# Where the last reciprocal roots of an RMSNorm are computed: on VectorE behind each tile, or on GpSimd between tiles

## The chip, the core and the metric

The kernel runs on one core of a Trainium2 chip (trn2). The metric is the time of one execution on the device, in microseconds. The core has five engines that run their own instruction streams and meet at semaphores: TensorE (PE, with its weight loads as PEld), VectorE (DVE), ScalarE (ACT), GpSimd (POOL) and SyncE (SP, which here only issues transfers). GpSimd issues transfers too.

## What is computed

One layer with a token-mixing half and an MLP half, 1024 tokens by 1024 channels, all in float32. The change touches only the last two lines, and of them only the end:

```python
def rmsnorm(x, g):
    y = x * lax.rsqrt(jnp.mean(x * x, axis=-1, keepdims=True) + EPS)
    return y * g

h = rmsnorm(x, g_mlp_pre)
f = jnp.square(jax.nn.relu(h @ w_up)) @ w_down
x = x + rmsnorm(f, g_mlp_post)
```

## The kernel before

Everything is written by hand: each engine's stream is a Python block, and each wait names a semaphore and a count. The tokens stand in eight tiles of 128 rows. The product with `w_down` is accumulated over the hidden channels in the on-chip tile `acc` (128 x 8 x 1024). The last slice of hidden channels is multiplied in at the very end, in 16 products of a tile `t` with a half of 512 output columns `s`, in the order of the list `LAST_DOWN`: (0,0), (1,0), (2,0), (0,1), (1,1), (2,1), and then (3,0), (3,1), (4,0) and so on to (7,1). This text calls them product 0 to product 15. Each is 12 matmuls on PE into one of eight banks.

For each product the other engines do the following.

- DVE adds the bank to `acc` (the **add**, line 2033), then writes `acc * 32 * gain` to a buffer of weighted values (the **mul**, line 2038). The buffer is `yx`, a view of `yst`, with room for two tiles.
- ACT squares the same half of `acc` and sums the squares of a row into a column of `sumsq` (line 1242). It is started by the add.
- When both halves of a tile are there, DVE computes the reciprocal root of the row's sum of squares: an integer seed and three Newton steps on columns of one or two numbers per partition (the **root**, lines 2010 to 2019). Each instruction waits for the one before it. Tiles 0 to 5 are done in pairs, tiles 6 and 7 singly; all of this is the function `finish`.
- DVE then writes `weighted * root + x1` into a third of `tok` (the **out**, line 2024). The residual `x1` of tile `t` has been brought there by a transfer that GpSimd issues (`x1_load`, line 767). There are three such places, so that the load for tile `t` waits until the output of tile `t - 3` has been sent (`out_sent`).
- SP sends the tile to the output (line 577). The last tile's out and its transfer are in two halves.

PE never waits for any of this in the last 16 products, since a bank is free again long before it comes round.

Of the kernel before, what the change touches and what calls it, by code (L numbers as in the profile page):

```python
# [17 lines left out]
D = 1024  # L18
L = 1024
KT = D // P  # L20
NT = L // P
# [8 lines left out]
EPS = 1e-6  # L30
# [26 lines left out]
RSQRT_SEED = float(0x5F3759DF)  # L57
# [63 lines left out]


LAST_DOWN = [(0, 0), (1, 0), (2, 0), (0, 1), (1, 1), (2, 1)] + [(t, s) for t in range(3, 8) for s in range(2)]


UP_PRODUCTS = [("uP1", 0, 0), ("uP2", 1, 1), ("uP6", 3, 2), ("uP5", 2, 3), ("uP7", 4, 0), ("uP3", 5, 1), ("uP4", 6, 2)]
# [33 lines left out]
def hybrid_layer(nc, a, out):  # L160
    f32, f32r, i32 = mybir.dt.float32, mybir.dt.float32r, mybir.dt.int32
    ALU, ACT, AX = mybir.AluOpType, mybir.ActivationFunctionType, mybir.AxisListType
    add, sub, mul = ALU.add, ALU.subtract, ALU.mult
    ctx = ExitStack()
    with ctx:
# [3 lines left out]
        def sem(name):  # L169
            return ctx.enter_context(nc.semaphore(name))  # L170
# [10 lines left out]
        stat = sb("stat", [P, 8])  # L181
        rs = sb("rs", [P, 10])
        sumsq = sb("sumsq", [P, 40])
        mx = sb("mx", [P, 64])
# [7 lines left out]
        raw = sb("raw", [P, 2, UNIT])  # L192
# [5 lines left out]
        tok = sb("tok", [P, 4096])  # L198
        yst = sb("yst", [P, 4, 512])
# [132 lines left out]
        sq_f = sem("sq_f")  # L332
# [8 lines left out]
        third_in = [sem(f"third_in{h}") for h in range(2)]  # L341
        turn_used = sem("turn_used")
        step_made, step_hi, step_lo, step_out = sem("step_made"), sem("step_hi"), sem("step_lo"), [sem(f"step_out{k}") for k in range(2)]
        x1_back = [sem(f"x1_back{s}") for s in range(3)]
        out_made, out_sent = sem("out_made"), [sem(f"out_sent{s}") for s in range(3)]
        chain = sem("chain")
# [127 lines left out]
        def loaded(slot, u, it):  # L474

            return w_loaded[slot], 16 * (2 * ((u - U_QX) // 2 + 1) + 2) + it * 64


        @block.sync
# [107 lines left out]
        def _(pool):  # L587

            g = nc.gpsimd
# [102 lines left out]
            yx = yst[:, :, :].rearrange("p (s a) c -> p s (a c)", s=2)  # L692
# [73 lines left out]
            def x1_load(t):  # L766
                g.dma_start(tok[:, (1 + t % 3) * D:(2 + t % 3) * D], x1_dram[tile_of(t) * P:(tile_of(t) + 1) * P, :]).then_inc(x1_back[t % 3], 16)
# [3 lines left out]
            x1_load(2)  # L771
            pool.wait_ge(f_lo, 8 + 42 + 4)
            x1_load(0)
            for t in range(3, NT):
                pool.wait_ge(out_sent[t % 3], 16 * (t // 3))
                x1_load(t)


        @block.scalar
# [467 lines left out]
        def _(dve):  # L1247
            V = nc.vector
            issued = [0]

            def mark(ins):

                issued[0] += 1
                ins.then_inc(chain, 1)

            def settle():

                dve.wait_ge(chain, issued[0])

            def do(ins):  # L1260
                mark(ins)
                settle()
# [71 lines left out]
            for e in range(2):  # L1334
                for idx in range(2):
                    n = norm_event(idx, e)
# [63 lines left out]
            for i, e in enumerate(X_ORDER):  # L1400
                n = FIRST["xsc"] + i
# [6 lines left out]
                                       in1=m2.unsqueeze(2).to_broadcast([P, 2, MEM]), op0=mul, op1=sub).then_inc(bank_free[n % 8], 1)  # L1408
# [34 lines left out]
            for i in range(2, 7):  # L1443
                rope(i)
                if i > 4:
                    n = FIRST["kv"] + i - 3
# [4 lines left out]
            for q in range(8):  # L1451
                for m in range(2):
                    n = FIRST["xpv"] + pv_event(q, m)
# [7 lines left out]
            for e in range(16):  # L1461
# [4 lines left out]
                n = score_event(e)  # L1466
                j = e % 2
# [5 lines left out]
                for lo, hi, nk in parts:  # L1473
# [4 lines left out]
                                          scalar=SS, in1=sk, op0=mul, op1=ALU.max))  # L1478
                for lo, hi, nk in parts:
                    ins = V.scalar_tensor_tensor(out=pe4[:, lo:hi, 0:nk], in0=ps[:, lo:hi, 0:nk], scalar=SS,  # L1480
                                                 in1=m4[:, lo:hi].unsqueeze(2).to_broadcast([P, hi - lo, nk]), op0=mul, op1=sub)
# [33 lines left out]
            for k in (1, 2, 4):  # L1515
                o = [pwF[:, ri, :, k + 1:2 * k + 1] for ri in range(2)]
                x = [pwF[:, ri, :, 1:k + 1] for ri in range(2)]
                y = [pwF[:, ri, :, k].unsqueeze(2).to_broadcast([P, NPAIR, k]) for ri in range(2)]
                t = [tt[:, 0:NPAIR * k].rearrange("p (a b) -> p a b", b=k) for tt in temps]
# [31 lines left out]
            for q in range(8):  # L1551
                n = FIRST["spv"] + spv_event(q, 2)
# [32 lines left out]
            for r in range(4):  # L1585
# [22 lines left out]
                for k in range(1, 7):  # L1608
                    w = 1 << k
# [5 lines left out]
                for e in range(2):  # L1615
                    n = FIRST[f"s5a{r}"] + 4 + e
                    wait_full(dve, n)
                    q = slice(2 * e, 2 * e + 2)
                    w = [banks[n % 8][:, :].rearrange("p (a ri c) -> p ri a c", a=2, ri=2)[:, ri] for ri in range(2)]
                    t = [tt[:, 256 * e:256 * e + 256].rearrange("p (a b) -> p a b", a=2) for tt in temps]  # L1620
# [19 lines left out]
                for e in range(2):  # L1640
                    n = FIRST[f"s5m{r}"] + e
                    dve.wait_ge(s5_even, 2 * r + e + 1)
                    for m in range(4):
# [3 lines left out]
                        ins = V.scalar_tensor_tensor(out=dst, in0=odd, scalar=parity[rows, 1:2], in1=dst, op0=mul, op1=add)  # L1647
# [6 lines left out]
                for e in range(2):  # L1654
                    n = FIRST[f"s5y{r}"] + e
# [19 lines left out]
            for e in range(8):  # L1675
                n = FIRST["yg"] + e
# [4 lines left out]
            for s in range(2):  # L1681
                prep_lo(dve, U_MERGE_A + s + 1)
                for j in range(8):
                    n, d, h = FIRST["mergeA"] + 8 * s + j, 4 * s + j // 2, slice((j % 2) * 512, (j % 2) * 512 + 512)
# [10 lines left out]
            for s in range(2):  # L1695
                prep_lo(dve, U_GLU + s + 1)
                for j in range(4):
                    n = FIRST["glu"] + 8 * s + 2 * j
                    h = slice((j % 2) * 512, (j % 2) * 512 + 512)
# [12 lines left out]
            for b, (stage, u) in enumerate((("mergeM", U_MERGE_M), ("mergeS", U_MERGE_S))):  # L1712
                dve.wait_ge(merged, 16 * (b + 1))
                for s in range(2):
                    prep_lo(dve, u + s + 1)
                    for j in range(8):
                        n, d, h = FIRST[stage] + 8 * s + j, 4 * s + j // 2, slice((j % 2) * 512, (j % 2) * 512 + 512)
# [63 lines left out]
            def step(i):  # L1781

                which, half = STEPS[i]
                b11, b12, b21, b22 = ([quarter(y, k, t, half) for y in (hThi, hTlo)] for k in range(2) for t in range(2))
                out, t2 = step_sum(i), tok_part[half]
                if which == S_T3:
                    do(V.tensor_tensor(out, b22[0], b12[0], sub))
                    do(V.tensor_tensor(out, out, b22[1], add))
                    V.tensor_tensor(out, out, b12[1], sub).then_inc(step_made, 1)
                elif which == S_T2:  # L1790
                    dve.wait_ge(step_lo, half + 1)
                    do(V.tensor_tensor(out, out, b11[0], add))
                    V.tensor_tensor(out, out, b11[1], add).then_inc(step_made, 1)
                else:
                    dve.wait_ge(step_lo, i)
                    first, then = (b22 if which == S_T1 else b21)
                    if i < 5:
                        dve.wait_ge(step_out[1], 32)
                    do(V.tensor_tensor(out, first, t2, sub))
                    V.tensor_tensor(out, out, then, add).then_inc(step_made, 1)  # L1800
# [200 lines left out]
                down_phase(m)  # L2001
            up_phase(6, True)

            def finish(tiles):

                c, n = slice(tiles[0], tiles[-1] + 1), len(tiles)
                v, nv, y, w = (stat[:, 2 * k:2 * k + n] for k in (0, 1, 2, 3)) if n == 1 else \
                    (stat[:, 0:2], stat[:, 2:4], rs[:, 0:2], stat[:, 4:6])
                dve.wait_ge(sq_f, LAST_DOWN.index((tiles[-1], 1)) + 1)
                do(V.scalar_tensor_tensor(out=v, in0=sumsq[:, 26:34][:, c], scalar=D * EPS, in1=sumsq[:, 10:18][:, c], op0=add, op1=add))  # L2010
                mark(V.tensor_scalar(nv, v, -0.5, None, mul))
                do(V.tensor_scalar(y.bitcast(i32), v.bitcast(i32), -0.5, RSQRT_SEED, mul, add))
                for _ in range(3):
                    if n == 1:
                        do(V.scalar_tensor_tensor(out=w, in0=y, scalar=nv, in1=y, op0=mul, op1=mul))
                    else:
                        do(V.tensor_tensor(w, y, y, mul))
                        do(V.tensor_tensor(w, w, nv, mul))
                    do(V.scalar_tensor_tensor(out=y, in0=w, scalar=1.5, in1=y, op0=add, op1=mul))
                for k, t in enumerate(tiles):  # L2020
                    xt = tok[:, (1 + t % 3) * D:(2 + t % 3) * D]
                    dve.wait_ge(x1_back[t % 3], 16 * (t // 3 + 1))
                    for h in ([slice(0, D)] if t < NT - 1 else [slice(0, 512), slice(512, D)]):
                        V.scalar_tensor_tensor(out=xt[:, h], in0=yx[:, t % 2, h], scalar=y[:, k:k + 1], in1=xt[:, h], op0=mul, op1=add)\  # L2024
                            .then_inc(out_made, 1)

            dve.wait_ge(last_gain, 16)
            n_last = F + 24
            for i, (t, s) in enumerate(LAST_DOWN):
                n, h = n_last + i, slice(s * 512, s * 512 + 512)  # L2030
                wait_full(dve, n)
                a = acc[:, tile_of(t), :]
                V.tensor_tensor(a[:, h], banks[n % 8][:, :], a[:, h], add).then_inc(bank_free[n % 8], 1)  # L2033
                wait_taken(dve, n)
                if (t, s) == (2, 0):
                    continue
                h = slice(0, D) if t == 2 else h
                mark(V.scalar_tensor_tensor(out=yx[:, t % 2, h], in0=a[:, h], scalar=float(D) ** 0.5, in1=tok[:, h],
                                            op0=mul, op1=mul))
                if s == 1 and t in (1, 3, 5):  # L2040
                    finish((t - 1, t))
                elif s == 1 and t > 5:
                    finish((t,))


        @block.tensor
# [491 lines left out]
```

## Time and profile before

| | |
|---|---|
| median of three runs | 1471.96 us (1471.65 to 1472.15) |
| span of the profiled execution, first to last instruction | 1470.3 us |
| its own time beside the span | not listed apart; the runs' median is 1.7 us above the span |
| granted TensorE clock over the span | 0.998 of full speed |
| first of the 16 last products begins, last one ends (PE) | 1416.50 us, 1460.28 us |
| last add begins on DVE | 1463.11 us |

All moments in this document are microseconds from the start of the span of the profiled execution. A row of the timeline gives the start, the duration, the engine and the line, what is written and what is read, and in brackets how long the engine had been idle and what ended that. "L2033" is line 2033 of the kernel before. An instruction that waits for nothing can start before the one ahead of it has wholly ended, so that the distance between starts is a little less than the duration.

### The profile page before, as it was taken

Reading aid. Unit: us, or ns where it says so; the run is one execution under the profiler, and the core shown is the slowest. Engines: PE = TensorE matmul, PEld = TensorE weight load, DVE = VectorE, ACT = ScalarE, POOL = GpSimd, SP = SyncE. Lnnn points to the kernel's source line nnn. Section 1 sums busy time; section 2 is a strip of 40 time slices with the busy share of each in tenths; the row PEclk is TensorE's granted clock in tenths of the full one; section 3 lists DMA queues with packets and bytes.
Section 4 is the critical chain, followed back from the end, with each engine's and each line's share of the span. In section 5 each row is a group of like instructions: output and inputs, shape, how many; then the busy total and the mean of one; then the engine's idle time right before and its main releaser. Section 6 shows DMA issues by size and latency. Waiting matters only on the chain.

```text
span 1470.3 us, 18474 instructions
## 1 busy us (share of the span) xinstructions
PE 1453.1 (99%) x7110; PEld 1210.6 (82%) x7110; DVE 1077.3 (73%) x1754; ACT 537.9 (37%) x697; POOL 198.8 (14%) x299
## 2 busy tenths in 40 slices
PE   8999999999999999999999999999999999999997
PEld 7888888888888888888898888888888888888885
DVE  6778668658757735446756869697969697978878
ACT  4445853323132253221234432333334343434332
POOL 0000010140211112101100212302020201011110
PEclk9999999999999999999999999999999999999999
DMA  8301120242213246424433436937372736464545
GB/s 329 73 29 58 58 87 29 100 130 95 73 64 107 65 135 206 146 68 133 172 102 113 129 115 207 308 114 229 98 242 88 228 115 208 134 180 145 168 165 186
DMA packets 113890, 199.65 MB, mean 136 GB/s; under 512 B 15224, under 2 KB 57248, under 8 KB 113824
## 3 DMA queue, kind: packets, MB, share of 16 engines
q0 software_dynamic: 46256, 118.53, 25.6%
q1 hardware_dynamic: 67552, 80.23, 16.5%
q8 instruction: 43, 0.70, 0.2%
q14 instruction: 23, 0.19, 0.0%
q10 hardware_dynamic: 16, 0.00, 0.0%
HBM read 163.08 MB, written 35.65 MB: 135 GB/s over the span
## 4 chain that ended last, share of the span: by engine, by line
PE 92%; DVE 5%; DMA 1%; issue 1%; ACT 1%; DVEq 0%; SPq 0%; ACTq 0%
PE bank L2056 53%; PE bank L2465 17%; PE bank L2485 14%; PE bank L2066 3%; PE bank L2096 1%; PE bank L2158 1%; DMA raw<-in_w_down_dram 1%; DVE tok L2024 1%; PE bank L2321 1%; PE bank L2306 1%; PE bank L2326 1%; PE bank L2291 1%; PE bank L2208 1%; PE bank L2263 1%; DVE acc L2033 1%
## 5 line engine op out<-in xcount | busy, mean ns | idle before, releaser
L2056 PE MATMUL bank<-hThi,whi 128*128 128x512 f32 x736 | 289.4, 393 | 0.1
L2056 PE MATMUL bank<-hThi,wlo 128*128 128x512 f32 x736 | 286.6, 389 | 0.0
L2056 PE MATMUL bank<-hTlo,whi 128*128 128x512 f32 x736 | 286.5, 389 | 0.0
L2056 PEld LDWEIGHTS bank<-hThi,whi 128*128 128x128 f32 x736 | 138.1, 188 | 30.1 <-issue 1.1
L1125 ACT ACTIVATE whi<-raw 128x1024 fp32r<-128x1024 f32 x91 | 95.3, 1055 | 183.4 <-DVE raw L1860 97.8
L2056 PEld LDWEIGHTS bank<-hThi,wlo 128*128 128x128 f32 x736 | 138.1, 188 | 29.2
L2056 PEld LDWEIGHTS bank<-hTlo,whi 128*128 128x128 f32 x736 | 138.2, 188 | 27.9
L1850 DVE TENSOR_TENSOR wlo<-raw,whi 128x1024 fp32r<-128x1024 f32 x91 | 111.0, 1220 | 33.6 <-ACT whi L1125 33.6
L2465 PE MATMUL bank<-hThi,whi 128*128 128x512 f32 x336 | 130.8, 389 | 0.5 <-DMA hTlo<-h_scratch 0.5
L2485 PE MATMUL bank<-whi,yhi 128*128 128x512 f32 x336 | 130.8, 389 | 0.4 <-DVE acc L1883 0.4
L2465 PE MATMUL bank<-hThi,wlo 128*128 128x512 f32 x336 | 130.7, 389 | 0.0
L2465 PE MATMUL bank<-hTlo,whi 128*128 128x512 f32 x336 | 130.7, 389 | 0.0
L2485 PE MATMUL bank<-whi,ylo 128*128 128x512 f32 x336 | 130.7, 389 | 0.0
L2485 PE MATMUL bank<-wlo,yhi 128*128 128x512 f32 x336 | 130.7, 389 | 0.0
L378 ACT ACTIVATE whi<-raw 128x2048 fp32r<-128x2048 f32 x32 | 61.2, 1916 | 102.8 <-PE bank L2056 70.3
L384 DVE TENSOR_TENSOR wlo<-raw,whi 128x2048 fp32r<-128x2048 f32 x33 | 75.5, 2290 | 18.1 <-ACT whi L378 17.4
L1883 DVE TENSOR_TENSOR acc<-bank,acc 128x1024 f32<-128x1024 f32 x72 | 86.1, 1218 | 1.0 <-PE bank L2485 1.0
L924 ACT ACTIVATE scr<-bank 128x512 f32<-128x512 f32 x48 | 28.5, 598 | 157.0 <-PE bank L2056 141.9
L2465 PEld LDWEIGHTS bank<-hThi,whi 128*128 128x128 f32 x336 | 63.1, 188 | 14.1 <-DMA hTlo<-h_scratch 0.9
L2485 PEld LDWEIGHTS bank<-whi,yhi 128*128 128x128 f32 x336 | 63.0, 188 | 13.8 <-DVE acc L1883 0.8
L2485 PEld LDWEIGHTS bank<-whi,ylo 128*128 128x128 f32 x336 | 63.1, 188 | 13.2
L2465 PEld LDWEIGHTS bank<-hThi,wlo 128*128 128x128 f32 x336 | 63.1, 188 | 13.1
(412 smaller groups left out, 2764.8 us busy)
## 6 DMA issues: line engine op xcount, KB each, us to landing
hThi<-h_scratch POOLq DMA_DIRECT2D x42, 512.0 KB, 5.3
hTlo<-h_scratch POOLq DMA_DIRECT2D x42, 512.0 KB, 6.5
raw<-in_w_in_dram SPq DMA_DIRECT2D x34, 512.0 KB, 4.7
raw<-in_w_up_dram SPq DMA_DIRECT2D x32, 512.0 KB, 4.2
raw<-in_w_down_dram SPq DMA_DIRECT2D x32, 512.0 KB, 4.5
gate_scratch<-scr POOLq DMA_DIRECT2D x48, 256.0 KB, 2.3
tok<-gate_scratch POOLq DMA_DIRECT2D x24, 512.0 KB, 3.6
yhi<-h_scratch POOLq DMA_DIRECT2D x14, 512.0 KB, 5.8
```

Source lines behind the costliest of these rows:

```text
L378: nc.scalar.activation(parts(u)[0], raw[:, u % 2, :], ACT.Copy).then_inc(w_hi, 1)
L384: nc.vector.tensor_tensor(lo, raw[:, u % 2, :], hi.bitcast(f32), sub).then_inc(w_lo, 1)
L924: A.activation(scr[:, gp % 2, :], banks[n % 8][:, :], ACT.Sigmoid).then_inc(bank_free[n % 8], 1)
L1125: A.activation(w_slot(whi, place), source, ACT.Copy).then_inc(w_hi, 1)
L1850: V.tensor_tensor(w_slot(wlo, place), source, w_slot(whi, place).bitcast(f32), sub).then_inc(w_lo, 1)
L1883: V.tensor_tensor(dst[:, 2 * h:2 * h + 2, :], pair_banks(k), dst[:, 2 * h:2 * h + 2, :], add).then_inc(pair_free[k], 1)
L2024: V.scalar_tensor_tensor(out=xt[:, h], in0=yx[:, t % 2, h], scalar=y[:, k:k + 1], in1=xt[:, h], op0=mul, op1=add)\
L2033: V.tensor_tensor(a[:, h], banks[n % 8][:, :], a[:, h], add).then_inc(bank_free[n % 8], 1)
L2056: ins = T.matmul(dst, lhs(k)[p], rhs(k)[q], start=start and k == 0 and i == 0, stop=stop and k == kt - 1 and i == 2)
L2066: ins = T.transpose(banks[n % 8][:, i * P:i * P + P] if dsts is None else dsts[i], src, by)
L2465: ins = T.matmul(banks[2 * k + c][:, :], w[:, kk, c * P:c * P + P], x[:, kk, :], start=opens and kk == 0 and i == 0, stop=kk == 3 and i == ...
L2485: ins = T.matmul(banks[2 * k + t % 2][:, :], x[:, kk, rows], w[:, kk, :], start=opens and kk == 0 and i == 0, stop=kk == 1 and i == 2, ski ...
```

## The change

There are three parts.

1. The roots of tiles 0 to 6 are computed by GpSimd (`make_root`), in groups of tiles (0, 1), (2, 3), (4, 5) and (6). Each is 15 instructions, and each of these waits on the semaphore `root_step` for the one before it. Their numbers stand in columns of `mx`. GpSimd's stream has one order: the first two groups, the loads of `x1` for tiles 3, 4 and 5, the third group, the load for tile 6, the fourth group, the load for tile 7. Tile 7's root stays on DVE.
2. Weighted values of tiles 2 to 5 go to the weight buffer `raw`, which is free by then; tiles 0, 1, 6 and 7 stay in `yst`. Tile 2 is multiplied in two halves rather than in one piece.
3. The outs are set between products by the table `OUT_AFTER`: tile 0 after product 6, tile 1 after 7, tile 2 after 9, tile 3 after 10, tile 4 after 12, tile 5 after 13, tile 6 after 14. Each waits for its `x1` and for `root_step` to reach 15, 30, 45 or 60.

```diff
+ROOTS = [(0, 1), (2, 3), (4, 5), (6,)]
+ROOT_STEPS = 15
+OUT_AFTER = {6: 0, 7: 1, 9: 2, 10: 3, 12: 4, 13: 5, 14: 6}
...
+        def last_rows(t):
+
+            return yst[:, 2 * (t % 2):2 * (t % 2) + 2, :].rearrange("p a c -> p (a c)") if t < 2 or t > 5 else \
+                raw[:, (t - 2) // 2, (t % 2) * D:(t % 2) * D + D]
...
-            for t in range(3, NT):
+            def step(ins):
+
+                roots[0] += 1
+                ins.then_inc(root_step, 1)
+                pool.wait_ge(root_step, roots[0])
+
+            def make_root(k):
+
+                tiles = ROOTS[k]
+                v, nv, y, w = root(k)
+                c = slice(tiles[0], tiles[-1] + 1)
+                pool.wait_ge(sq_f, LAST_DOWN.index((tiles[-1], 1)) + 1)
+                step(g.tensor_tensor(v, sumsq[:, 26:34][:, c], sumsq[:, 10:18][:, c], add))
+                step(g.tensor_scalar(v, v, D * EPS, None, add))
+                step(g.tensor_scalar(y.bitcast(i32), v.bitcast(i32), -0.5, RSQRT_SEED, mul, add))
+                for _ in range(3):
+                    step(g.tensor_tensor(w, y, y, mul))
+                    step(g.tensor_tensor(w, w, v, mul))
+                    step(g.tensor_scalar(w, w, -0.5, 1.5, mul, add))
+                    step(g.tensor_tensor(y, w, y, mul))
+
+            def x1_again(t):
+
                 pool.wait_ge(out_sent[t % 3], 16 * (t // 3))
                 x1_load(t)
+
+            make_root(0)
+            make_root(1)
+            x1_again(3)
+            x1_again(4)
+            x1_again(5)
+            make_root(2)
+            x1_again(6)
+            make_root(3)
+            x1_again(7)
...
-                if (t, s) == (2, 0):
-                    continue
-                h = slice(0, D) if t == 2 else h
-                mark(V.scalar_tensor_tensor(out=yx[:, t % 2, h], in0=a[:, h], scalar=float(D) ** 0.5, in1=tok[:, h],
-                                            op0=mul, op1=mul))
-                if s == 1 and t in (1, 3, 5):
-                    finish((t - 1, t))
-                elif s == 1 and t > 5:
-                    finish((t,))
+                mark(V.scalar_tensor_tensor(out=last_rows(t)[:, h], in0=a[:, h], scalar=float(D) ** 0.5, in1=tok[:, h], op0=mul, op1=mul))
+                if i in OUT_AFTER:
+                    done = OUT_AFTER[i]
+                    k = done // 2
+                    dve.wait_ge(root_step, ROOT_STEPS * (k + 1))
+                    settle()
+                    out_rows(done, root(k)[2][:, done % 2:done % 2 + 1])
+            y7 = last_root(NT - 1)
+            settle()
+            out_rows(NT - 1, y7)
```

How DVE's stream stands in the built programs, around the outs of tiles 4 and 5. Here L2024 is the out, L2033 the add, L2038 the mul, and L2017 to L2019 the end of a root. Before:

```order
L2017 TENSOR_TENSOR stat<-rs 128x2 [waits chain]
L2018 TENSOR_TENSOR stat<-stat 128x2 [waits chain]
L2019 SCALAR_TENSOR_TENSOR rs<-stat,rs 128x2 [waits chain]
L2024 SCALAR_TENSOR_TENSOR tok<-yst,rs,tok 128x1024 [waits x1_back1,chain]
L2024 SCALAR_TENSOR_TENSOR tok<-yst,rs,tok 128x1024 [waits x1_back2]
L2033 TENSOR_TENSOR acc<-bank,acc 128x512 [waits bank_full5]
L2038 SCALAR_TENSOR_TENSOR yst<-acc,tok 128x512 [waits bank_free5]
L2033 TENSOR_TENSOR acc<-bank,acc 128x512 [waits bank_full6]
L2038 SCALAR_TENSOR_TENSOR yst<-acc,tok 128x512 [waits bank_free6]
```

In the changed program the out is L2074, the add L2083 and the mul L2085; this is the stream from product 12 to product 14:

```order
L2083 TENSOR_TENSOR acc<-bank,acc 128x512 [waits bank_full5]
L2085 SCALAR_TENSOR_TENSOR yst<-acc,tok 128x512 [waits bank_free5]
L2074 SCALAR_TENSOR_TENSOR tok<-raw,mx,tok 128x1024 [waits x1_back1,chain,root_step]
L2083 TENSOR_TENSOR acc<-bank,acc 128x512 [waits bank_full6]
L2085 SCALAR_TENSOR_TENSOR yst<-acc,tok 128x512 [waits bank_free6]
L2074 SCALAR_TENSOR_TENSOR tok<-raw,mx,tok 128x1024 [waits x1_back2,chain,root_step]
L2083 TENSOR_TENSOR acc<-bank,acc 128x512 [waits bank_full7]
L2085 SCALAR_TENSOR_TENSOR yst<-acc,tok 128x512 [waits bank_free7]
L2074 SCALAR_TENSOR_TENSOR tok<-yst,mx,tok 128x1024 [waits x1_back0,chain,root_step]
```

The root's instructions have left DVE; each out now stands alone behind an add and a mul, and waits for `root_step`, which GpSimd counts up.

GpSimd's stream from the load of tile 0's `x1` on, before (L767 is `x1_load`):

```order
L767 DMA tok<-x_scratch 128x1024 [waits f_lo]
L767 DMA tok<-x_scratch 128x1024 [waits out_sent0]
L767 DMA tok<-x_scratch 128x1024 [waits out_sent1]
L767 DMA tok<-x_scratch 128x1024 [waits out_sent2]
L767 DMA tok<-x_scratch 128x1024 [waits out_sent0]
L767 DMA tok<-x_scratch 128x1024 [waits out_sent1]
```

And in the changed program, from the end of the second group of roots to the beginning of the third (L785 is `x1_load`, L807 to L814 a root):

```order
L813 TENSOR_SCALAR mx<-mx 128x2 [waits root_step]
L814 TENSOR_TENSOR mx<-mx 128x2 [waits root_step]
L785 DMA tok<-x_scratch 128x1024 [waits out_sent0,root_step]
L785 DMA tok<-x_scratch 128x1024 [waits out_sent1]
L785 DMA tok<-x_scratch 128x1024 [waits out_sent2]
L807 TENSOR_TENSOR mx<-sumsq 128x2 [waits sq_f]
L808 TENSOR_SCALAR mx<-mx 128x2 [waits root_step]
L809 TENSOR_SCALAR mx<-mx 128x2 [waits root_step]
L811 TENSOR_TENSOR mx<-mx 128x2 [waits root_step]
```

The loads of `x1` now stand behind roots in GpSimd's one stream, and the third root stands behind a load that waits for the output of tile 2.

## Rows read from the trace of the kernel before

**Rows 1.** Windows: busy time of each engine in stretches of the end.

```profile
core 0: us, PE busy (x) PEld busy (x) DVE busy (x) ACT busy (x) POOL busy (x), PEclk, DMA share, GB/s
1430.00:1440.00 10.00, 10.00 (x46) 8.29 (x45) 9.05 (x21) 2.17 (x6) 0.53 (x1) 1.00 0.29 111
1440.00:1450.00 10.00, 10.00 (x46) 8.29 (x45) 9.41 (x23) 2.90 (x8) 1.59 (x3) 1.00 0.65 231
1450.00:1460.00 10.00, 10.00 (x46) 8.18 (x44) 9.21 (x27) 2.17 (x6) 0.53 (x1) 1.00 0.60 209
```

**Rows 2.** Timeline of PE: the first and the last matmuls of the 192.

```profile
1416.50 0.47 PE L2056 MATMUL bank<-whi,yhi 128*128 128x512 f32 x1
...
1459.66 0.39 PE L2056 MATMUL bank<-wlo,yhi 128*128 128x512 f32 x1
1459.89 0.39 PE L2056 MATMUL bank<-whi,ylo 128*128 128x512 f32 x1
```

**Rows 3.** Timeline of DVE: the roots of tiles 4, 5 and the last product.

```profile
1451.35 0.16 DVE L2010 SCALAR_TENSOR_TENSOR stat<-sumsq 128x2 f32<-128x2 f32 x1
...
1453.19 0.16 DVE L2018 TENSOR_TENSOR stat<-stat 128x2 f32<-128x2 f32 x1
1453.39 0.16 DVE L2019 SCALAR_TENSOR_TENSOR rs<-stat,rs 128x2 f32<-128x2 f32 x1
1453.59 2.48 DVE L2024 SCALAR_TENSOR_TENSOR tok<-yst,rs,tok 128x1024 f32<-128x1024 f32 x2
...
1463.11 0.68 DVE L2033 TENSOR_TENSOR acc<-bank,acc 128x512 f32<-128x512 f32 x1
1463.83 0.69 DVE L2038 SCALAR_TENSOR_TENSOR yst<-acc,tok 128x512 f32<-128x512 f32 x1
1464.58 0.16 DVE L2010 SCALAR_TENSOR_TENSOR stat<-sumsq 128x1 f32<-128x1 f32 x1
...
1466.37 1.42 DVE L2024 SCALAR_TENSOR_TENSOR tok<-yst,stat,tok 128x512 f32<-128x512 f32 x2
```

**Rows 4.** Timeline of ACT: the squares of one product.

```profile
1450.59 0.63 ACT L1242 ACTIVATE scr<-acc 128x512 f32<-128x512 f32 x1 [0.60 <-DVE acc L2033]
1451.13 0.19 ACT L1242 ACTIVATION_READ_ACCUMULATOR scr<-acc 128x1 f32 x1
```

**Rows 5.** Groups of GpSimd's instructions: count, busy time, mean ns, idle before.

```profile
L641 POOL TENSOR_TENSOR tok<-tok,Dbc 128x1024 f32<-128x1024 f32 x4 | 10.4, 2598 | 14.3 <-ACT uT L786 14.3
L593 POOL TENSOR_SCALAR_AFFINE_SELECT ident<-ident 128x128 f32<-128x128 f32 x1 | 0.3, 289 | 0.2 <-POOL halfpi L591 0.2
L590 POOL MEMSET ident<- 128x128 f32 x1 | 0.2, 205 | 0.3 <-POOLq L2523 0.3
L591 POOL MEMSET halfpi<- 128x1 f32 x1 | 0.1, 99 | 0.0
```

**Rows 6.** Timeline at 377 us: GpSimd works beside DVE.

```profile
376.92 1.09 ACT L786 ACTIVATE uT<-bank 128x512 f32<-128x512 f32 x2 [3.75 <-PE bank L2066]
377.09 5.11 DVE L1595 TENSOR_TENSOR t<-yst,cpk 128x512 f32<-128x512 f32 x4
378.16 2.47 POOL L641 TENSOR_TENSOR tok<-tok,Dbc 128x1024 f32<-128x1024 f32 x1 [4.15 <-ACT uT L786]
```

**Rows 7.** Source L1595: durations in ns, min/median/max.

```profile
L1595 DVE TENSOR_TENSOR t<-yst,cpk x16: 681/690/2899, 324.2 to 488.3; 128x512 f32<-128x512 f32 x16
```

**Rows 8.** Timeline of GpSimd and SP: the `x1` loads and the outputs.

```profile
1435.43 26.80 SPq L577 DMA_DIRECT2D out_dram<-tok  x7
1438.46 0.53 POOL L767 DMA_DIRECT2D tok<-x_scratch  x1 [15.38 <-DMA out_dram<-tok]
1457.78 0.53 POOL L767 DMA_DIRECT2D tok<-x_scratch  x1 [8.32 <-DMA out_dram<-tok]
```

**Rows 9.** DMA issues after 1420 us: KB each, median us to landing.

```profile
out_dram<-tok SPq DMA_DIRECT2D x7, 512.0 KB, 2.6
tok<-x_scratch POOLq DMA_DIRECT2D x6, 512.0 KB, 3.6
```

More of the change, by code:

```diff
@@ L343, in hybrid_layer @@
         step_made, step_hi, step_lo, step_out = sem("step_made"), sem("step_hi"), sem("step_lo"), [sem(f"step_out{k}") for k in range(2)]
+        root_step = sem("root_step")
         x1_back = [sem(f"x1_back{s}") for s in range(3)]
@@ L476, in loaded, with root @@
             return w_loaded[slot], 16 * (2 * ((u - U_QX) // 2 + 1) + 2) + it * 64
+        def root(k):
+            c = mx[:, 8 * k:8 * k + 8]
+            n = len(ROOTS[k])
+            return [c[:, 2 * j:2 * j + n] for j in range(4)]
+        def last_rows(t):
+            return yst[:, 2 * (t % 2):2 * (t % 2) + 2, :].rearrange("p a c -> p (a c)") if t < 2 or t > 5 else \
+                raw[:, (t - 2) // 2, (t % 2) * D:(t % 2) * D + D]
         @block.sync
@@ L773, in _ @@
             x1_load(0)
-            for t in range(3, NT):
+            roots = [0]
+            def step(ins):
[16 more added lines that the diff above has]
+            def x1_again(t):
                 pool.wait_ge(out_sent[t % 3], 16 * (t // 3))
                 x1_load(t)
+            make_root(0)
[7 more added lines that the diff above has]
+            x1_again(7)
         @block.scalar
@@ L2002, in _, with last_root @@
             up_phase(6, True)
[L2004 to L2010, printed above, removed]
+            def last_root(t):
+                v, nv, y, w = (stat[:, k:k + 1] for k in range(4))
+                dve.wait_ge(sq_f, LAST_DOWN.index((t, 1)) + 1)
+                do(V.scalar_tensor_tensor(out=v, in0=sumsq[:, 26 + t:27 + t], scalar=D * EPS, in1=sumsq[:, 10 + t:11 + t], op0=add, op1=add))
                 mark(V.tensor_scalar(nv, v, -0.5, None, mul))
@@ L2013, in finish, with out_rows @@
                 for _ in range(3):
[L2014 to L2018, printed above, removed]
-                    do(V.scalar_tensor_tensor(out=y, in0=w, scalar=1.5, in1=y, op0=add, op1=mul))
[L2020 to L2025, printed above, removed]
+                    do(V.scalar_tensor_tensor(out=w, in0=y, scalar=nv, in1=y, op0=mul, op1=mul))
+                    do(V.scalar_tensor_tensor(out=y, in0=w, scalar=1.5, in1=y, op0=add, op1=mul))
+                return y
+            def out_rows(t, y):
+                xt = tok[:, (1 + t % 3) * D:(2 + t % 3) * D]
+                dve.wait_ge(x1_back[t % 3], 16 * (t // 3 + 1))
+                for h in ([slice(0, D)] if t < NT - 1 else [slice(0, 512), slice(512, D)]):
+                    V.scalar_tensor_tensor(out=xt[:, h], in0=last_rows(t)[:, h], scalar=y, in1=xt[:, h], op0=mul, op1=add)\
+                        .then_inc(out_made, 1)
             dve.wait_ge(last_gain, 16)
```

## The prediction

> **What bounds the kernel now.** I read the stretches of the end first. From 1430 to 1460 us PE is busy without a gap, at the full granted clock, and DVE is busy 9.05, 9.41 and 9.21 us of each 10 [rows 1]. Both look full, so the timeline decides. PE's 192 matmuls of the last 16 products run from 1416.50 to 1459.89 + 0.39 = 1460.28 us, with nothing between them [rows 2]; that is (1460.28 - 1416.50) / 16 = 2.7 us for a product. DVE begins the last add at 1463.11 us, 2.8 us after its bank was full [rows 3]. So PE bounds the stretch until DVE falls behind, and the last 2.8 us are DVE's arrears. Behind the last add comes a chain that the change leaves alone: add, squares on ACT, tile 7's root, two half outs, their transfers, 1470.3 - 1463.1 = 7.2 us.
>
> This gives the ceiling. DVE cannot begin the last add before about 1460.35 us. **The most the change can win is 2.8 us, 0.19% of 1472.** About 0.2% (2.9 us) is also what a measurement of this kernel can tell from no change. A clear win is all but excluded before any cost is counted.
>
> **What leaves DVE.** A pair's root runs from 1451.35 to the out at 1453.59: 2.24 us, in 12 instructions, a step every 0.2 us [rows 3]. Three pairs and tile 6's single root (9 instructions, a little under 1.8 us as tile 7's takes, 1464.58 to 1466.37) are 8.5 us. The squares' share of the wait between mul and root goes too. DVE then needs 0.72 (add) + 0.61 (mul) + 1.2 (out) = 2.55 us for a product with an out, under PE's 2.7 us. The distances between starts are 1463.83 - 1463.11 for the add and half of 2.48 us for an out [rows 3]; the mul's 0.69 us duration overlaps the next start by 0.08. Tile 2's mul in two halves costs 0.1 us more, and is hidden behind PE. The place of the weighted values (`raw` or `yst`) costs nothing by itself. It only lets roots be late without stopping the muls.
>
> **What a root costs on GpSimd.** 15 instructions, each waiting for the one before. The trace has no such small operation there, so I bound a step from both sides, as duration plus the time until the next can begin.
>
> - Duration: a memset of one column takes 0.099 us and one of 128 columns 0.205, so the columns cost 0.106 of that. The select over 128 columns, which also reads, takes 0.289 [rows 5]: less the columns' 0.106, 0.18 us for an instruction that reads and writes. Low end 0.10, high end 0.29.
> - Until the next begins: ACT's two copies end at 376.92 + 1.09 = 378.01 and GpSimd's instruction that waits for them starts at 378.16 [rows 6]: 0.15 us. Low end 0.04, DVE's own (0.20 between starts less 0.16 us). High end 0.24, the idle time between two dependent GpSimd instructions, in which the sequencer also did something else [rows 5].
>
> So a step lies between 0.14 and 0.53 us. I take 0.18 + 0.15 = 0.33, since both come from instructions that read a tile or wait for another engine, as these do. A root is then 15 x 0.33 = 5.0 us alone, against 2.24 on DVE.
>
> **GpSimd and DVE hold each other up.** Four DVE instructions with both inputs in SBUF take 5.11 us beside GpSimd's multiply of 2.47 us [rows 6]. Alone one takes 0.68; the longest took 2.90 [rows 7]. The surplus, 2.2 us, is nearly GpSimd's whole instruction. The mul and the out are such DVE instructions; the add reads a bank and one SBUF tile. I let muls and outs hold a GpSimd step until they end (0.61 and 1.2 us), and a running step hold them. Adds I leave free, and keep the other way as a bound.
>
> The Trainium skill, "SBUF — State Buffer", section "Who interferes with whom", states it as an exclusive lock: a DVE instruction with two SBUF inputs contends with a GpSimd instruction that reads SBUF. The rows above agree; by the same page an add would stay free.
>
> **The sum.** I lay both streams in program order on the time axis: full banks every 2.72 us as now, squares 0.83 us after the mul begins (1450.59 to 1451.13 and 0.19 for reading the sum, with the hop to the reader 0.83) [rows 4], GpSimd's issue 0.53 us, a load landed 3.6 us after its issue [rows 9], `out_sent` 2.9 us after an out ends. The last is 2.6 us of transfer [rows 9] plus the hops; now 1438.46 less 1435.43 is 3.0 us [rows 8].
>
> | group | root runs | first out that needs it | DVE was free at |
> |---|---|---|---|
> | 0, 1 | 1431.9 to 1437.8 | 1437.9 | 1437.3 |
> | 2, 3 | 1440.6 to 1447.5 | 1447.6 | 1445.4 |
> | 4, 5 | 1453.8 to 1459.4 | 1459.5 | 1454.9 |
> | 6 | 1462.2 to 1468.5 | 1468.6 | 1464.7 |
>
> A root is now 5.6 to 6.9 us long. Two queues add to it. The load for tile 3 stands behind the second root: issued 1447.5, landed 1451.1, and DVE, free at 1450.1, waits 1.0 us. The third root stands behind the load for tile 5, which waits for tile 2's output (1448.8 + 2.9 = 1451.7), so little is lost there; the squares of product 11 come at 1453.8 only because DVE is late by then. The third root is asked for after one product, the fourth at once. Both can't be ready, and DVE, which is the engine in arrears, stands still 4.6 and 3.9 us. Behind the waiting out on DVE stand the next add and mul, and behind the add the squares that the next root waits for: lateness is passed on. The last add begins at 1469.8 instead of 1463.1. Tile 7's load, behind the fourth root, is issued at 1468.5 and lands at 1472.1, before its out at 1473.1; it has 1 us to spare.
>
> 1469.8 - 1463.1 = +6.7 us. The profiled span is 1470.3 and the median of the runs 1471.96: 1.7 us stand around the span, and they stay. Forecast: 1472.0 + 6.7 = **1478.7 us**.
>
> **How it hangs on the step**, by the same layout, with the hold and (in brackets) without: 0.14 us: -1.7 (-2.7); 0.20: +0.1 (-1.9); 0.24: +2.3 (-0.7); 0.33: +6.7 (+2.4); 0.40: +11 (+6); 0.53: +18 (+14). With adds held too, 0.33 gives +11.
>
> **Rivals.**
>
> 1. *The roots keep up* (chance 0.12). If a step is under 0.18 us, a root ends within a product, DVE's arrears go, and the time falls by 1.3 to 2.8 us, to about 1469.8: the other side, though hardly beyond what can be measured. For it: the one-column memset, 0.099 us [rows 5], and DVE's steps of 0.2. Against it: that memset reads nothing. It decides from a step of 0.20 us downwards with the hold, 0.26 without.
> 2. *About even* (0.18). Steps of 0.2 to 0.25 us: the gain on DVE is eaten by short waits at the outs of tiles 4 and 6. 1472 to 1474.8, say 1473.5.
> 3. *Tiny steps hold nothing up* (0.10). The hold was seen on instructions of 0.7 and 2.5 us; two columns may slip between. With a step of 0.33: 1472.0 + 2.4 = 1474.4.
> 4. *Dearer steps, or adds held too* (0.15). 0.40 us and up, or 0.33 with adds held: +11 to +17, say 1485. A two-input instruction may cost more than a one-input one. GpSimd's multiply of 1024 columns takes 2474 ns at the least [rows 6]; it gives no bound on the fixed part by itself.
>
> The Trainium skill, "GPSIMD Engine Reference", section "3.1 Elementwise — side-by-side cycle accounting", gives 4497 ns for a two-input add of 2048 columns. With this trace's 2474 ns for 1024 the line has a fixed part of 0.45 us: an estimate. Ten of the 15 steps have two inputs, and by that they would be 0.60 us each and a root 7.7 us, for about +17 us, rival 4. No run here shows such a small instruction yet.
>
> **How the numbers follow.** The forecast's own case, steps of 0.28 to 0.40 us with the hold, has 0.45 and its own range is 1475.5 to 1483. The 80% range leaves out half of rival 4 and the better half of rival 1: 1470.3 to 1484. Slower by over 0.2% (over 1474.9): the forecast's case, rival 4 and a part of rival 3, 0.63. Faster by over 0.2% needs more than the ceiling of 2.8 us: 0.03. Within it: 0.34.
>
> **What the changed profile would show.** GpSimd's rows of `mx`: their start-to-start distance is the step, and one that is longer beside a DVE mul or out is the hold. DVE's out of tiles 2, 4 and 6 idle before it, released by GpSimd; the out of tile 3 by a load. PE's last matmul still at 1460.3. The last add at 1469.8. If DVE is idle nowhere after 1437 us and the last add begins at 1460.4, step and hold were both mis-sized, and rival 1 holds. If the idle time stands before outs and is ended by transfers, the order of the loads is the cause and not the step.

## The result and the profile after

The changed kernel takes 1477.57 us (median of 5), before in the same series 1471.65 us: ratio 1.0040, 95% interval 1.0029 to 1.0051, so 4.3 to 7.5 us slower. The forecast was 1478.7. All medians in this document are of fast runs; one run of the experiment early_loads, which took 2099.78 us at a granted clock of 0.655 in place of 0.997, is left out.

DVE's timeline from product 6 on, in excerpts ("..." marks rows left out):

```profile
1436.31 0.69 DVE L2085 SCALAR_TENSOR_TENSOR raw<-acc,tok 128x512 f32<-128x512 f32 x1
1437.11 1.28 DVE L2074 SCALAR_TENSOR_TENSOR tok<-yst,mx,tok 128x1024 f32<-128x1024 f32 x1
...
1439.82 1.28 DVE L2074 SCALAR_TENSOR_TENSOR tok<-yst,mx,tok 128x1024 f32<-128x1024 f32 x1
...
1441.75 0.69 DVE L2085 SCALAR_TENSOR_TENSOR raw<-acc,tok 128x512 f32<-128x512 f32 x1
1443.74 0.69 DVE L2083 TENSOR_TENSOR acc<-bank,acc 128x512 f32<-128x512 f32 x1 [1.30 <-PE bank L2107]
...
1446.07 1.28 DVE L2074 SCALAR_TENSOR_TENSOR tok<-raw,mx,tok 128x1024 f32<-128x1024 f32 x1 [0.91 <-POOL mx L814]
...
1451.02 1.29 DVE L2074 SCALAR_TENSOR_TENSOR tok<-raw,mx,tok 128x1024 f32<-128x1024 f32 x1 [2.33 <-DMA tok<-x_scratch]
...
1458.93 1.28 DVE L2074 SCALAR_TENSOR_TENSOR tok<-raw,mx,tok 128x1024 f32<-128x1024 f32 x1 [3.97 <-POOL mx L814]
1460.13 0.68 DVE L2083 TENSOR_TENSOR acc<-bank,acc 128x512 f32<-128x512 f32 x1
1460.85 0.69 DVE L2085 SCALAR_TENSOR_TENSOR yst<-acc,tok 128x512 f32<-128x512 f32 x1
1461.64 1.28 DVE L2074 SCALAR_TENSOR_TENSOR tok<-raw,mx,tok 128x1024 f32<-128x1024 f32 x1
1462.85 0.68 DVE L2083 TENSOR_TENSOR acc<-bank,acc 128x512 f32<-128x512 f32 x1
...
1467.08 1.29 DVE L2074 SCALAR_TENSOR_TENSOR tok<-yst,mx,tok 128x1024 f32<-128x1024 f32 x1 [2.82 <-POOL mx L814]
1468.28 0.68 DVE L2083 TENSOR_TENSOR acc<-bank,acc 128x512 f32<-128x512 f32 x1
...
1471.88 1.42 DVE L2074 SCALAR_TENSOR_TENSOR tok<-yst,stat,tok 128x512 f32<-128x512 f32 x2 [0.36 <-DMA tok<-x_scratch]
```

The outs of tiles 2, 4 and 6 wait 0.9, 4.0 and 2.8 us for a root from GpSimd, those of tiles 3 and 7 wait 2.3 and 0.4 us for their `x1`. The last add begins at 1468.28, where before it began at 1463.11 [rows 3]. The add of product 9 at 1443.74 is the last that waits for its bank: there DVE has caught up with PE, so that all it owes at the end comes from later waits.

GpSimd's timeline: the first root's beginning, then parts of the other three.

```profile
1431.68 0.19 POOL L807 TENSOR_TENSOR mx<-sumsq 128x2 f32<-128x2 f32 x1 [8.86 <-ACT scr L1295]
1431.97 0.23 POOL L808 TENSOR_SCALAR mx<-mx 128x2 f32<-128x2 f32 x1
1432.28 0.19 POOL L809 TENSOR_SCALAR mx<-mx 128x2 int32<-128x2 int32 x1
1432.55 0.19 POOL L811 TENSOR_TENSOR mx<-mx 128x2 f32<-128x2 f32 x1
1432.82 0.19 POOL L812 TENSOR_TENSOR mx<-mx 128x2 f32<-128x2 f32 x1
...
1439.89 1.27 POOL L807 TENSOR_TENSOR mx<-sumsq 128x2 f32<-128x2 f32 x1 [3.63 <-ACT scr L1295]
...
1441.82 0.68 POOL L811 TENSOR_TENSOR mx<-mx 128x2 f32<-128x2 f32 x1
...
1445.84 0.19 POOL L814 TENSOR_TENSOR mx<-mx 128x2 f32<-128x2 f32 x1
1446.33 1.13 POOL L785 DMA_DIRECT2D tok<-x_scratch  x2 [0.30 <-POOL mx L814]
1454.12 0.53 POOL L785 DMA_DIRECT2D tok<-x_scratch  x1 [6.66 <-DMA out_dram<-tok]
1454.66 0.35 POOL L807 TENSOR_TENSOR mx<-sumsq 128x2 f32<-128x2 f32 x1
...
1461.66 0.18 POOL L807 TENSOR_TENSOR mx<-sumsq 128x1 f32<-128x1 f32 x1 [1.86 <-ACT scr L1295]
1461.94 1.07 POOL L808 TENSOR_SCALAR mx<-mx 128x1 f32<-128x1 f32 x1
```

A step is 0.19 us long and the next begins 0.275 us after it began (1432.82 less 1432.55 is 0.27). Some take 0.68 and 1.27 us. The step of 1.27 us began at 1439.89, as DVE's out of tile 1 ran from 1439.82 to 1441.10; the one of 0.68 us at 1441.82, beside the mul of product 8.

The chain that ended last, in order of time, one stretch of it:

```profile
1446.07 1.30 DVE tok L2074
1447.38 6.45 DMA out_dram<-tok
1453.84 0.28 issue
1454.12 0.53 POOL tok L785
1454.66 0.36 POOL mx L807
```

Tile 2's out, its way to the output, the load that waits for it and the third root form one chain. The root doesn't need that load (it is for tile 5); it only stands behind it in GpSimd's one stream. The transfer took 6.5 us, where those of before took 2.6 in the median [rows 9].

**A measure free of what lies ahead.** The runs of a kernel scatter by a microsecond or two, and a single profile shares that: PE's last matmul ends at 1460.28 us before [rows 2], at 1459.63 + 0.39 = 1460.02 in the changed kernel, and at 1462.5 and 1462.8 in two experiments. The tail, from that end to the end of the span, is then the better measure for a profile. It is 1470.3 - 1460.28 = 10.0 us before and 1475.8 - 1460.02 = 15.8 us after: +5.8 us, as the medians have it (+5.9). Of the 5.8 us, 5.4 lie ahead of the last add (8.26 us behind PE's end, 2.83 before) and 0.4 in the wait for tile 7's load. The tail scatters too: the two controls below, which can't be told from the kernel before, have 9.5 and 9.9.

### The profile page after: what moved, and what is told of

The parts are those of the page before. It is cut to its first block, busy times and chain, and to the rows that moved or that the text cites. A ratio compares the mean times of both kernels' runs of the same rounds, so it can differ in the third digit from the quotient of the medians.

```text
span 1475.8 us, 18496 instructions
## 1 busy us (share of the span) xinstructions
PE 1453.0 (98%) x7110; PEld 1210.7 (82%) x7110; DVE 1071.1 (73%) x1710; ACT 538.2 (36%) x697; POOL 214.4 (15%) x359
## 4 chain that ended last, share of the span: by engine, by line
PE 92%; DVE 3%; DMA 2%; issue 1%; POOL 1%; ACT 1%; DVEq 0%; SPq 0%; POOLq 0%; ACTq 0%
PE bank L2107 53%; PE bank L2516 17%; PE bank L2536 14%; PE bank L2117 3%; PE bank L2147 1%; PE bank L2209 1%; DMA raw<-in_w_down_dram 1%; PE bank L2357 1%; PE bank L2372 1%; PE bank L2377 1%; PE bank L2342 1%; PE bank L2259 1%; PE bank L2314 1%; DMA out_dram<-tok 0%; DVE tok L2074 0%
```

## The experiments

| run | median us | ratio (95%) | end of PE, tail us |
|---|---|---|---|
| before | 1471.44 to 1471.65 in four series | 1 | 1460.28, 10.0 |
| changed | 1477.57 | 1.0040 (1.0029 to 1.0051) | 1460.02, 15.8 |
| early_loads | 1475.07 | 1.0024 (1.0014 to 1.0034) | 1462.80, 13.0 |
| dve_roots | 1474.39 | 1.0017 (1.0008 to 1.0026) | 1459.38, 12.2 |
| two_newton | 1472.91 | 1.0010 (1.0001 to 1.0019) | 1459.56, 11.8 |
| no_hold | 1475.39 | 1.0030 (1.0018 to 1.0042) | 1459.21, 14.0 |
| buffers_only | 1471.13 | 0.9997 (0.9988 to 1.0006) | 1460.50, 9.5 |
| before_early_loads | 1471.55 | 1.0005 (0.9996 to 1.0014) | 1459.78, 9.9 |
| early_late | 1472.11 | 1.0004 (0.9995 to 1.0013) | 1461.02, 10.0 |
| mixed | 1472.99 | 1.0012 (1.0003 to 1.0022) | 1462.54, 11.3 |
| pair_67 | 1470.89 | 0.9995 (0.9986 to 1.0004) | 1459.58, 9.4 |
| pool_6_only | 1470.86 | 0.9998 (0.9989 to 1.0007) | 1459.89, 9.2 |

The changed kernel was measured in one series and the experiments in three others. Since the kernel before agrees to 0.2 us in all four, medians are compared across them.

**early_loads.** The loads leave the place behind the roots, and nothing waits for an output. The residuals of tiles 3 to 7 go to a free part of `hThi`, their outs to `acc`; that part of the edit is left out here.

```diff
+            for t in range(3, NT):
+                pool.wait_ge(x1_back[t % 3], 16 * (t // 3))
+                x1_load(t)
...
             make_root(0)
             make_root(1)
-            x1_again(3)
-            x1_again(4)
-            x1_again(5)
             make_root(2)
-            x1_again(6)
             make_root(3)
-            x1_again(7)
```

> The changed kernel, but the residuals of tiles 3 to 7 are loaded into the free space of hThi right behind tile 0's load, and their outs go to acc; no load stands behind a root and none waits for an output. Theory (both the length of a root, 15 steps of 0.275 us, and the loads queued behind roots are on the path): the outs of tiles 3 and 7 no longer wait, the third root begins with the squares of product 11, and what is left is the three late roots; last add near 1465.6 instead of 1468.3, time 1474.3 us (1473.5 to 1475.3). Rival (the loads are innocent, roots alone set the end): 1477.5. Rival (the loads alone do the harm): at or under 1471.5.

Measured 1475.07, near the upper edge of what was expected and 2.5 us under the changed kernel; the tail is 2.8 us shorter. The waits of its end:

```profile
POOL mx L821 <- ACT scr L1304: 11.2, 3, 5.5
DVE acc L2092 <- PE bank L2116: 7.0, 6, 1.3
DVE acc L2083 <- POOL mx L828: 5.9, 2, 3.1
...
DVE tok L2083 <- POOL mx L828: 0.9, 1, 0.9
```

DVE waits for no load any more, and still 6.8 us for roots (7.7 in the changed kernel). So both rivals fall: the loads carried 2.5 to 2.8 of the 5.9 us. That late roots carry the rest is not shown by this run alone; early_late below shows it.

**dve_roots.** Roots back on DVE, each right before the first out that needs it, in the old form; the loads stand in one run (left out here).

```diff
-                    dve.wait_ge(root_step, ROOT_STEPS * (k + 1))
+                    if done % 2 == 0:
+                        pair_root(k)
```

> The changed kernel with its buffers and its table of outs, but each root computed on VectorE right before the first out that needs it, in the old form (12 and 9 instructions), and the loads in one run on GpSimd as before. Theory (GpSimd's steps do the harm): VectorE never waits for a root or a load, its work is that of before, set later; laid out, the last add begins near 1464.6: 1473.1 us (1471.8 to 1474.0). Rival (the other buffers, tile 2 in two halves or the table of outs do the harm): near 1477.

1474.39: 3.2 us under the changed kernel, but 2.8 over before, outside of the range that I gave. The waits name the reason. First DVE's two waits for PE in the kernel before, then the group of them here (us in all, times, longest):

```profile
1427.75 0.69 DVE L2033 TENSOR_TENSOR acc<-bank,acc 128x512 f32<-128x512 f32 x1 [2.10 <-PE bank L2056]
...
1430.40 0.69 DVE L2033 TENSOR_TENSOR acc<-bank,acc 128x512 f32<-128x512 f32 x1 [1.23 <-PE bank L2056]
```

```profile
DVE acc L2093 <- PE bank L2118: 5.2, 4, 1.3
```

Before, DVE waits for PE twice, 3.3 us in all; here four times, 5.2 us, because the first root and outs are set behind product 6 rather than behind product 4. DVE idles 1.9 us more where it had work it could do, and is that much later at the end: the last add begins 1464.36 - 1459.38 = 5.0 us behind PE, 2.8 before. That is most of the tail's 2.2 us. So the table of outs costs some 2 us by itself when DVE still has the roots.

**two_newton.** Two Newton steps on GpSimd in place of three, so that the roots are less exact.

```diff
-                for _ in range(3):
+                for _ in range(2):
                     step(g.tensor_tensor(w, y, y, mul))
```

> The changed kernel with two Newton steps instead of three in the roots on GpSimd, so that its roots are less exact: 11 steps instead of 15. Theory (three roots are on the path, each step counts 0.275 us in each): 3 x 4 x 0.275 = 3.3 us less and a little less held: 1474.0 us (1473.2 to 1475.0). Rival (fixed costs of handing a root over, or the loads, set the time): 1476.5 to 1477.6.

1472.91, 4.7 us under the changed kernel (tail 4.0 less) and a little beyond the range. Four steps less in a root are 1.1 us, and three roots on the path make 3.3; holds and `x1` waits (2.7 us there, 1.3 here) shrink with them. Against the rival, the length of the chain of steps is on the path to the end.

**no_hold.** The mul reads the bank rather than `acc`; what `acc` held is missing in the values. The squares on ACT are started by the add, as before.

```diff
-                mark(V.scalar_tensor_tensor(out=last_rows(t)[:, h], in0=a[:, h], scalar=float(D) ** 0.5, in1=tok[:, h], op0=mul, op1=mul))
+                V.scalar_tensor_tensor(out=last_rows(t)[:, h], in0=banks[n % 8][:, :], scalar=float(D) ** 0.5, in1=tok[:, h], op0=mul, op1=mul)\
+                    .then_inc(bank_free[n % 8], 1)
```

> The changed kernel, but the mul reads the bank (and the gain) instead of acc, so that only one of its inputs is in SBUF; the weighted values lack what acc held before. Theory (a VectorE instruction with two SBUF inputs holds a GpSimd step until it ends): the steps of 0.68 us in GpSimd's rows are gone, those beside an out (1.07 to 1.27 us) stay, each root that met a mul is 0.5 to 1 us shorter: 1475.6 us (1474.8 to 1476.6). Rival (the long steps have another cause): the 0.68 us steps stay and the time is 1477.5.

1475.39, 2.2 us under the changed kernel, as expected. Not all of it need be the hold: the mul also begins 0.60 us behind its add here, 0.72 in the changed kernel. GpSimd's timeline at the second root:

```profile
1439.08 1.14 POOL L807 TENSOR_TENSOR mx<-sumsq 128x2 f32<-128x2 f32 x1 [4.10 <-ACT scr L1295]
1440.30 0.21 POOL L808 TENSOR_SCALAR mx<-mx 128x2 f32<-128x2 f32 x1
1440.60 0.19 POOL L809 TENSOR_SCALAR mx<-mx 128x2 int32<-128x2 int32 x1
1440.87 0.20 POOL L811 TENSOR_TENSOR mx<-mx 128x2 f32<-128x2 f32 x1
...
1443.92 0.20 POOL L814 TENSOR_TENSOR mx<-mx 128x2 f32<-128x2 f32 x1
```

The step beside the out still takes 1.14 us; beside the mul of product 8 (DVE at 1440.81) it is 0.20. Every step of 0.68 us is gone from the four roots, as expected. The timelines also show that adds hold nothing, which answers a bound of the prediction: in the changed kernel's own, the add of 1432.86 to 1433.55 has steps of 0.19 and 0.20 us beside it.

**buffers_only and before_early_loads.** Two controls on the kernel before: the weighted values of tiles 2 to 5 in `raw`, and the loads into `hThi`.

> The kernel before with the second part of the change alone: weighted values of tiles 2 to 5 in raw, tile 2 multiplied in two halves; roots and outs as before. Theory (this part costs and gives nothing): 1471.7 us, the same as before within 0.5. Rival (the new place or the extra instruction costs something, which would explain why the run with the roots back on VectorE came out 2.7 us over before): 1473 or more.

> The kernel before with the residuals of tiles 3 to 7 loaded early into hThi. Before waits for no load, so theory says 1471.7 us, the same within 0.5; it is the control for the runs with early loads. Rival (the early loads disturb the last products or the outs): 1473 or more.

Both can't be told from before. The buffers, tile 2 in two halves and the early loads cost nothing that can be measured, which leaves the order of roots and outs for the 2.8 us of dve_roots.

**early_late.** Early loads, and each out later than in the change.

```diff
-OUT_AFTER = {6: 0, 7: 1, 9: 2, 10: 3, 12: 4, 13: 5, 14: 6}
+OUT_AFTER = {6: 0, 7: 1, 10: 2, 11: 3, 13: 4, 14: 5}
...
             y7 = last_root(NT - 1)
+            dve.wait_ge(root_step, ROOT_STEPS * 4)
             settle()
+            out_rows(6, root(3)[2][:, 0:1])
             out_rows(NT - 1, y7)
```

> The changed kernel with early loads and each out one product later (tile 0 after product 6, 1 after 7, 2 after 10, 3 after 11, 4 after 13, 5 after 14, tile 6 behind the computing of tile 7's root). Theory (what hurts is that roots are asked for before their 15 steps of 0.275 us are through): the waits for roots shrink from 3 to 9 us in all to under 1, the last add begins when its bank is full; the out of tile 6 between root 7 and out 7 costs 1.2 us; laid out 1471.2 us (1470.3 to 1472.5). Rival (GpSimd's roots slow VectorE in some other way, by holding its instructions): still 1473.5 or more.

1472.11, not to be told from before (interval 0.9995 to 1.0013) and 3.0 us under early_loads: the loss is gone though all four roots are on GpSimd. The waits:

```profile
DVE acc L2092 <- PE bank L2118: 7.8, 6, 1.3
...
DVE acc L2083 <- POOL mx L828: 0.9, 1, 0.9
DVE acc L2083 <- DVE stat L2075: 0.2, 1, 0.2
```

One product of distance (for tile 6 a little more) took the root waits from 6.8 us to 0.9. This isolates the cause of what early_loads left: not that a root is slow on GpSimd, but that it is asked for too soon. What keeps this kernel from winning stands behind the last add. That add begins 0.9 us behind PE's end (1461.92 less 1461.02), 2.8 before; but tile 6's out now stands ahead of tile 7's, and from the last add to tile 7's out are 4.6 us where before had 3.3, and from there to the end 4.5 where before had 3.9.

**mixed.** Tiles 4 and 5 as a pair on DVE behind product 11, the others on GpSimd, tile 6's out after the last mul.

```diff
+                if i == 11:
+                    pair_root(2)
...
+            dve.wait_ge(root_step, ROOT_STEPS * 3)
+            settle()
+            out_rows(6, root(3)[2][:, 0:1])
             y7 = last_root(NT - 1)
```

> Early loads; roots of tiles 0 to 3 and of tile 6 on GpSimd, where there is time, the pair 4, 5 on VectorE right behind product 11's mul, tile 6's out after the last mul. Theory: VectorE keeps up with TensorE, the last add begins within 0.5 us of its full bank, tile 6's out adds about 2 us ahead of tile 7's root: 1470.9 us (1470.0 to 1472.0), the only one that may beat before. Rival: the root of tile 6, begun after product 13, is later than laid out (5 us and more, held by muls and outs), and the time is 1472 or more.

1472.99: a miss, the rival was right.

```profile
1460.74 1.20 POOL L821 TENSOR_TENSOR mx<-sumsq 128x1 f32<-128x1 f32 x1 [11.90 <-ACT scr L1303]
...
1466.83 1.28 DVE L2082 SCALAR_TENSOR_TENSOR acc<-yst,mx,hThi 128x1024 f32<-128x1024 f32 x1 [2.29 <-POOL mx L828]
```

Tile 6's root began at 1460.74 with a step of 1.20 us beside an out and was held twice more by muls; its last step ended near 1466.8. DVE stood 2.3 us for it, with tile 7's root behind the wait.

**pair_67 and pool_6_only.** Two tries at beating both kernels, from the kernel before: tiles 6 and 7 as a pair on DVE; or tile 6's root alone on GpSimd.

```diff
-                if s == 1 and t in (1, 3, 5):
-                    finish((t - 1, t))
-                elif s == 1 and t > 5:
-                    finish((t,))
+                if s == 1 and t in (1, 3, 5, 7):
+                    finish((t - 1, t))
```

The edit of pool_6_only: the root's 15 steps behind the last load on GpSimd, tile 6's out between tile 7's root and out on DVE.

```diff
+            step(g.tensor_tensor(v, sumsq[:, 26:34][:, c], sumsq[:, 10:18][:, c], add))
...
+                if tiles == (NT - 1,):
+                    dve.wait_ge(root_step, 15)
...
-                elif s == 1 and t > 5:
-                    finish((t,))
+            finish((NT - 1,))
```

> The kernel before with tiles 6 and 7 as a fourth pair on VectorE: tile 6's single root (1.8 us) and out no longer stand ahead of the last two adds, and the pair's root (2.24 us) and tile 6's out (1.2 us) come after them. Theory (the last 2.8 us are VectorE's arrears, so that what is taken from ahead of the last add counts until the arrears are gone): last add 2.8 us earlier, at its full bank, then 0.45 + 1.2 us more behind it: 1.1 us less, 1470.4 us (1469.8 to 1471.2). Rival (nothing to win at the end, since the work only changes its place): 1471.5 or more.

> The kernel before with tile 6's root alone on GpSimd, behind all loads, and tile 6's out between the computing of tile 7's root and tile 7's out. Theory (a root on GpSimd is free where its 4.2 to 5.2 us pass before it is asked for; here from the squares of product 13 at about 1458.2 to about 1463.5): last add at its full bank, out of tile 6 adds 1.2 us: 1.6 us less, 1469.9 us (1469.3 to 1470.9). Rival (the root is later than that, since muls and outs hold it): 1471 or more.

1470.89 and 1470.86. Both lie 0.6 us under before, with 1 inside the interval, so neither is shown faster. Each is inside its range, but 0.5 and 1.0 us above its point. The tails say where the rest went. DVE's timeline of pool_6_only:

```profile
1459.92 0.69 DVE L2058 TENSOR_TENSOR acc<-bank,acc 128x512 f32<-128x512 f32 x1 [0.38 <-PE bank L2080]
...
1463.42 1.28 DVE L2044 SCALAR_TENSOR_TENSOR tok<-yst,mx,tok 128x1024 f32<-128x1024 f32 x1 [0.26 <-POOL mx L796]
1464.62 1.41 DVE L2049 SCALAR_TENSOR_TENSOR tok<-yst,stat,tok 128x512 f32<-128x512 f32 x2
```

The arrears are gone: the last add begins with its bank. From there to the last out are 4.7 us, where before had 3.3, since tile 6's out stands between. From the last out to the end of the span are 1469.1 - 1464.6 = 4.5 us, where before had 1470.3 - 1466.4 = 3.9 [rows 3]; tile 6's 512 KB are sent just ahead of tile 7's halves. That the transfers share the queues there is an inference from these distances; no run separates them.

## Why the prediction was right, point by point

**What bounds the kernel; the ceiling.** Right. Of the 2.8 us of arrears, the two best versions took all away from the last add, and are 0.6 us under before in the time, which is within the noise.

**A step on GpSimd.** Set at 0.33 us (0.18 + 0.15), measured 0.275 (0.19 + 0.085). The duration was right to 0.01; the time until the next begins was too long; it had been read from a wait for another engine. Against 0.20 on DVE, the 15 steps are 4.1 us alone where DVE's 12 take 2.2. The prediction's other estimate, 0.60 us for a two-input step, is refuted: two-input and one-input steps take the same 0.19 us. It came from a line drawn through one figure of this trace and one of the Trainium skill, "GPSIMD Engine Reference", section 3.1; the page's own figure isn't touched by this, since no run here has so large an instruction.

**The hold.** Right in kind and place, shown by no_hold: mul and out hold a step until they end, adds don't. Roots measured from the first step's start to the last one's end: 4.6, 6.1, 4.2 and 5.4 us. They were forecast at 5.9, 6.9, 5.6 and 6.3: the step's error makes 0.8 us of each difference, and the rest of the first and third (0.5 and 0.6 us) is hold that the layout had and the trace has not. The other direction, a step that holds DVE, is not seen: muls take 0.69 us and outs 1.28 to 1.31 with steps beside them, where before had 0.69 and 1.28. The Trainium skill's rule ("SBUF — State Buffer", "Who interferes with whom") agrees with both, 1.27 us beside an out and 0.19 to 0.20 beside an add.

**A product with an out.** The prediction gave DVE 2.55 us for add, mul and out (its own terms add up to 2.53), under PE's 2.7. Measured are 2.72 us, from the add at 1460.13 to the one at 1462.85: the out waits for the mul ahead of it and begins 0.79 us behind it, not 0.61. So DVE wins nothing back in such a product, and a wait for a root stays owed. In early_late the 0.92 us waited at tile 4's out are still the 0.9 us by which the last add is late.

**The waits.** Forecast and measured: tile 0, 0.6 and none; tile 2, 2.2 and 0.9; tile 3 for its load, 1.0 and 2.3; tile 4, 4.6 and 4.0; tile 6, 3.9 and 2.8; tile 7's load, none and 0.4.

**The loads: the mis-sized term.** The load was taken to land in 3.6 us and an output to be sent in 2.9. With the loads of tiles 3 and 4 issued in one run at 1446.3 and tile 2's output at 1447.4, three transfers of 512 KB lay together: the loads took 4.6 and 5.6 us and the output 6.5. That they slowed each other is an inference; no run separates them. Where I wrote that little is lost behind tile 5's load, 1.0 us was: the third root began at 1454.66, the squares of product 11 ended at 1453.67. And product 11 itself was late by tile 3's load. early_loads gives the whole share: 2.5 to 2.8 of the 5.9 us.

**The sum.** Cheaper roots and dearer loads offset each other: +6.7 forecast, +5.9 measured. The forecast came closer than its terms did, and that is in part luck. Its own table has +2.3 for a step of 0.24 and +6.7 for 0.33; between them, 0.275 gives about +4.0 (an estimate), and the loads, sized too small, made up the rest. The step measured lies just outside the 0.28 to 0.40 us of the forecast's own case, nearer to rival 2 (0.20 to 0.25), whose 1472 to 1474.8 us the time refutes. Rival 1 fell with the step, rival 3 with the hold, rival 4 with both.

**What was not foreseen.** The table of outs leaves DVE idle 1.3 us each before products 3 to 6; before, DVE idles 3.3 us in all and does the first root and two outs in that stretch. The prediction's text says nothing of it. In dve_roots the idle time is lost, some 2 us. In the changed kernel it isn't part of the loss: the add of product 9 waits 1.30 us for its bank, so nothing was owed there, and early_late idles in the same places and ties with before.

## What to carry to other kernels

Before a chain of small dependent operations moves to another engine, multiply its steps by that engine's distance from start to start, and ask for the result only after that time has passed: here one product (2.7 us) of distance was worth 3 us. Add what can hold a step: 15 steps are 4.1 us alone and took 4.2 to 6.1. Count everything that the chain's engine has queued behind it, transfers above all, for they start late and then in a bunch. And work out the ceiling first: where the arrears are 2.8 us, no arrangement ahead of the last add wins more, and work moved behind it costs again.

## What the runs showed of the hardware

- A GpSimd instruction on one or two columns takes 0.19 us (0.18 to 0.23) with one or two inputs, f32 or int32, and a dependent one begins 0.275 us after it began; on VectorE 0.16 and 0.20.
- A GpSimd step that starts while VectorE runs an instruction with two SBUF inputs lasts until that one ends, even if the step has a single input and one column (1.07 us for `mx<-mx 128x1`). In the seven profiles with roots on GpSimd, 49 steps began so and 45 were held. The other four began 0.01 to 0.05 us behind VectorE's instruction and took 0.18 to 0.19 us, as at 1461.66 above; one that began 0.03 us behind, at 1444.50, was held. With one of VectorE's inputs in a bank none is held: 100 steps stood beside such an instruction, 0.18 to 0.23 us each.
- A transfer from GpSimd follows the last step of a root after 0.30 us of idle time, though it waits only for that step.
